# Key/value tiles inside the gated unit, query tiles in quarters inside attention, another load order, and the MLP's last up chunk moved off VectorE

## What is computed

```python
h = rms_norm(x, norm_mix_g)
z = h @ w_in                        # (B, S, 1024 q | 256 k | 256 v | 1024 value | 1024 gate)
q = rope(rms_norm(q, q_norm_g), pos);  k = rope(rms_norm(k, k_norm_g), pos)
a = attn(q, k, v, sinks)            # window of 128; the prompt in blocks of 128 queries
u = u_val * sigmoid(u_gate)         # gated unit
c = causal_dwconv(u, c_buf, conv_w, conv_b)          # 31 taps
c = silu(layer_norm(c, conv_ln_g, conv_ln_b))
x = x + concat(a, c) @ w_out
x = x + square(relu(rms_norm(x, norm_mlp_g) @ w_up)) @ w_down   # 2048 -> 8192 -> 2048
```

## Time and profile before

| | |
|---|---|
| median of 3 runs | 1556.63 us (1556.50 to 1557.89) |
| the profiled execution | 1554.67 us; span of its slowest core 1553.1 us |
| spans of the cores | 1545.5 to 1553.1 us, granted clock 0.963 to 0.967 |
| TensorE busy | 1409.0 us, 91% |
| VectorE, ScalarE, GpSimd busy | 688.5, 359.9, 267.0 us |
| last chain | TensorE 81%, VectorE 6%, ScalarE 3%, transfers 3% |

### The profile page before, as it was taken

The page is one execution under the profiler, slowest core; times in us unless marked ns, Lnnn a source line. Parts: engine busy times, 40 slices in busy tenths (PEclk is TensorE's granted clock), DMA queues, the critical chain, the costliest instruction groups (busy, mean ns, idle before and its releaser), DMA issues.

```text
span 1553.1 us, 22041 instructions; the slowest of 8 cores (1545.5 to 1553.1 us)
## 1 busy us (share of the span) xinstructions
PE 1409.0 (91%) x9006; PEld 868.7 (56%) x9006; DVE 688.5 (44%) x770; ACT 359.9 (23%) x516; POOL 267.0 (17%) x260
## 2 busy tenths in 40 slices
PE   4589978776989899999999999999999999999996
PEld 2356643332226555566666666666666666666664
DVE  2556634465331211253453453463463463463464
ACT  3356675344772222101001001001001001001000
POOL 0577712646000000101001001001001001001000
PEclk9899999889899999999999999999999999999998
DMA  9556420310453343745245255245245246246309
GB/s 247 127 82 109 82 41 5 50 12 28 110 122 55 55 71 52 122 82 90 47 82 92 46 82 95 42 82 96 40 82 97 40 82 97 40 82 101 60 17 217
DMA packets 52517, 122.75 MB, mean 79 GB/s; under 512 B 19215, under 2 KB 22543, under 8 KB 52395
## 3 DMA queue, kind: packets, MB, share of 16 engines
q0 software_dynamic: 43888, 91.07, 36.4%
q1 hardware_dynamic: 8531, 30.28, 6.9%
HBM read 203.42 MB, written 10.35 MB: 138 GB/s over the span
## 4 chain that ended last, share of the span: by engine, by line
PE 81%; DVE 6%; ACT 3%; issue 3%; DMA 3%; SPq 1%; POOL 1%; DVEq 0%; ACTq 0%; POOLq 0%
PE psum L529 81%; DVE arena L501 5%; ACT arena L497 2%; DMA arena<-xu 2%; ACT arena L691 1%; SPq L484 1%; DVE arena L673 1%; DMA arena<-wup 1%; POOL arena L501 1%; DVE arena L516 0%; PE psum L533 0%; ACT arena L515 0%; DVE arena L606 0%; DVEq L262 0%; DVE arena L522 0%
## 5 line engine op out<-in xcount | busy, mean ns | idle before, releaser
L529 PE MATMUL psum<-arena 128*128 128x343 bf16 (+7 forms) x8880 | 1398.4, 318 | 99.6 <-DVE arena L501 59.3
L529 PEld LDWEIGHTS psum<-arena 128*128 128x128 bf16 (+2 forms) x8880 | 859.4, 99 | 632.6 <-issue 183.7
L501 DVE TENSOR_TENSOR arena<-psum,arena 128x1029 f32<-128x1029 f32 (+9 forms) x396 | 397.4, 1019 | 302.8 <-PE psum L529 263.0
L501 DVE TENSOR_TENSOR arena<-arena 128x1029 bf16<-128x1029 bf16 (+5 forms) x160 | 175.3, 1095 | 371.5 <-ACT arena L497 363.6
L497 ACT ACTIVATE arena<-psum 128x1029 bf16<-128x1029 f32 (+8 forms) x157 | 121.1, 773 | 835.1 <-PE psum L529 832.4
L501 POOL TENSOR_TENSOR arena<-arena 128x256 f32<-128x256 f32 (+8 forms) x58 | 155.3, 2684 | 139.2 <-DVE arena L501 85.9
L484 POOL DMA_DIRECT2D arena<-wup x64 | 33.9, 530 | 817.1 <-PE psum L529 817.0
L497 ACT ACTIVATE arena<-arena 128x512 f32<-128x512 f32 (+13 forms) x181 | 121.2, 694 | 217.7 <-DVE arena L501 123.2
L673 DVE TENSOR_TENSOR arena<-psum,arena 32x264 bf16<-32x264 f32 x128 | 78.5, 613 | 58.6 <-PE psum L529 54.9
L691 ACT ACTIVATE arena<-psum,arena 32x256 f32<-32x256 f32 x128 | 91.1, 712 | 46.5 <-PE psum L529 43.4
L522 DVE TENSOR_REDUCE arena<-arena 128x4 f32<-128x256 bf16 (+4 forms) x20 | 16.3, 817 | 75.3 <-ACT arena L497 75.2
(11 more groups left out here) (13 smaller groups left out, 26.8 us busy)
## 6 DMA issues: line engine op xcount, KB each, us to landing
arena<-wup POOLq DMA_DIRECT2D x64, 512.0 KB, 6.7
arena<-wdn POOLq DMA_DIRECT2D x64, 512.0 KB, 13.8
arena<-xu SPq DMA_DIRECT2D x16, 530.0 KB, 23.3
arena<-xt SPq DMA_DIRECT2D x16, 514.0 KB, 5.7
yt<-arena SPq DMA_DIRECT2D x16, 514.0 KB, 9.2
arena<-wu POOLq DMA_DIRECT2D x16, 512.0 KB, 6.2
arena<-wo POOLq DMA_DIRECT2D x16, 512.0 KB, 6.2
arena<-wq POOLq DMA_DIRECT2D x16, 256.0 KB, 6.0
```

Of the source, the lines that this page charges most:

```text
L501: return P.add(eng, lambda e: e.tensor_tensor(out=out.ap, in0=in0.ap, in1=in1.ap, op=op), reads=[in0, in1], writes=[out])
L529: return P.add("pe", lambda e: e.matmul(out.ap, lhsT.ap, rhs.ap, start=start, stop=stop), reads=[lhsT, rhs], writes=[out])
```

## The change

- **Start.** The third and fourth weight blocks wait for x 10 and x 13. The first value block is copied to the f32 tile `V0` by ScalarE, and `glu_mul(0)` reads that. The four key/value weight loads move ahead of the loop.
- **Gated unit.** `glu_mul` comes in two halves with a K/V tile between them. In channel c, from 2 on: first half of `glu_mul(c-1)`, `kv_tile(c-2)`, second half, the gate's matmuls, the transposes `kv_tr(c-2)`, `glu_gate(c)`, `conv(c-1)`, the bands for c + 1, the value's matmuls. In channel 1, GpSimd's order is: SG product, K tables, bands 1, bands 2, Q tables. The chain is split into `chain1` (square, products, reduction, first sum) and `chain2` (root and the last products).
- **Between.** K/V tiles 6 to 9, `conv(7)` with its second half taken out by VectorE, query tile 9, cache loads, the `cvs` transfers on SP, `u_outputs` (its state transposes in two batches), query tiles 1 and 2 with the first layer norm statistic. `UTO`, `LB8`, `LSQ8`, `SGL`, `PT` and `REC` have new places.
- **Attention.** In block n: scores, a quarter of query tile n + 3, values and denominators, a quarter, the unit's end, one channel's layer norm, and the same for the second unit. Scores have three banks in a ring. The samples' attention goes in three pieces after blocks 2, 3 and 4, the sigmoids after blocks 5 and 6, `ln_mul` with the load of its `XT` tile after block 6 and at the end; then `XT` 8 to 15 are loaded, and the memset of `XT` follows.
- **Output projection.** All squares on ScalarE; the 16 contraction steps go in the order CT 0 to 3, AT 0 to 3, CT 4 to 7, AT 4 to 7.
- **MLP.** A group's last up chunk is squared on ScalarE and scaled on GpSimd; the down weights of a group are issued one by one with its up chunks.

The diff, cut:

```diff
-    SGL = [sb(O_XU + 14624 + 2080 * i, BF16, (NM,)) for i in range(8)]
+    SGL = [sb(O_XU + 12576 + 2080 * i, BF16, (NM,)) for i in range(4)]
+    PT = [sb(O_XU + 23584 + 1024 * i, BF16, (4, 128)) for i in range(8)]
+    REC = sb(O_XU + 31776, F32, (4, 128))
-    UTO = sb(O_XU + 8480, F32, (8, 128))
+    UTO = sb(O_XU + 18080, F32, (8, 128))
-    LB8 = sb(O_XU + 17696, BF16, (8, 343))
-    LSQ8 = sb(O_XU + 23200, BF16, (8, 343))
+    LB8 = sb(O_XU + 12576, BF16, (8, 343))
+    LSQ8 = sb(O_XU + 18080, BF16, (8, 343))
+    V0 = sb(O_TMP + 5952, F32, (NCOL,))
...
-    load_wu(after=[xl[8]])
-    load_wu(after=[xl[11]])
+    load_wu(after=[xl[10]])
+    load_wu(after=[xl[13]])
...
+    cp("act", lin352(V0), main3(av))
+    cp("act", V0((NU, NCOL)), av(2, (352, 356)))
...
+    for c in range(1, 8):
+        if c >= 2:
+            glu_mul(c - 1, acc3(1), 0)
+            kv_tile(c - 2, 6)
+            glu_mul(c - 1, acc3(1), 1)
+        u_block(pending.pop(0), acc3(0))
+        if c == 1:
+            halo_stats()
+            col_stats()
+        else:
+            kv_tr(c - 2, 7)
+        glu_gate(c, acc3(0))
+        load_wu()
+        if c == 1:
+            tt("pool", GCK(), TABIN(0), bc(GK, 1, (128, 10, 64)), ALU.mult)
+            tt("pool", GSK(), TABIN(1), bc(GKS, 1, (128, 10, 64)), ALU.mult)
+        conv(c - 1) if c >= 2 else None
+        if c == 1:
+            build_bands(1)
+        elif c + 1 < 8:
+            build_bands(c + 1) if c >= 2 else None
+        u_block(pending.pop(0), acc3(1))
+        if c == 1:
+            conv(0)
+            build_bands(2)
+            tt("pool", GCQ(), TABIN(0), bc(GQ, 1, (128, 10, 64)), ALU.mult)
+            tt("pool", GSQ(), TABIN(1), bc(GQS, 1, (128, 10, 64)), ALU.mult)
+        load_wu()
...
     def ln_mul(c):
-        tt("dve", CT(c), CC(c), SGL[c](), ALU.mult)
+        tt("dve", CT(c), CC(c), SGL[c % 4](), ALU.mult)
+        dma("sp", XT(c, (0, NX)), R(xt_d[c]), "xr%d" % c)
...
+    glu_mul(7, acc3(1), 0)
+    kv_tile(6, 0)
+    glu_mul(7, acc3(1), 1)
+    kv_tile(7, 1)
+    kv_tr(6, 2)
+    kv_tile(8, 0)
+    kv_tr(7, 2)
+    conv(7)
+    kv_tile(9, 1)
+    kv_tr(8, 2)
...
+    q_part(9, 3, 0, 16)
+    kv_tr(9, 2)
...
+    dma("pool", CKB(p=(0, 127)), R(ck[:, 1:128, :].rearrange("s k d -> k s d")), "cks", group=True)
+    dma("pool", CVB(p=(0, 127)), R(cv[:, 1:128, :].rearrange("s k d -> k s d")), "cks", group=True)
+    for s_ in range(SPC):
+        dma("sp", CVB(s_, p=(127, 128)), VB_S(p=(s_, s_ + 1)), "cvs", group=True)
+    q_chain1(9)
+    q_chain2(9)
+    u_outputs()
+    q_part(1, 0, 0, 16)
+    q_tr(9)
+    q_chain1(1)
+    ln_cast(0)
+    q_chain2(1)
+    q_part(2, 3, 0, 16)
+    ln_stats(0)
+    q_tr(1)
+    q_chain1(2)
+    ln_cast(1)
...
+    for n in range(8):
+        qn = n + 3 if n + 3 <= 8 else None
+        u0, u1 = 2 * n, 2 * n + 1
+        sc(u0)
+        if qn:
+            q_part(qn, 0, 0, 4)
+        if n == 0:
+            ln_stats(1)
+        if n + 2 <= 8:
+            q_chain2(n + 2)
+        pv(u0)
+        if qn:
+            q_part(qn, 0, 4, 8)
+        unit_b(u0)
+        if n == 0:
+            ln_cast(2)
+        elif n >= 2:
+            ln_step(2)
+        sc(u1)
+        if qn:
+            q_part(qn, 0, 8, 12)
+        if n + 2 <= 8:
+            q_tr(n + 2)
+        if n == 0:
+            ln_stats(2)
+        pv(u1)
+        if qn:
+            q_part(qn, 0, 12, 16)
+        unit_b(u1)
+        if n >= 1:
+            ln_step(2 if n < 6 else 2)
+        if qn:
+            q_chain1(qn)
...
+    for c in range(4, 8):
+        ln_mul(c)
+    for k in range(8, 16):
+        dma("sp", XT(k, (0, NX)), R(xt_d[k]), "xr%d" % k)
     memset("pool", XT((0, 16), (NM - 1, NM)), 0.0)
...
-        if dc % 4 != 3:
-            act(sq((0, 1024)), XT(dc, (0, 1024)), AF.Square)
-        else:
-            tt("dve", sq((0, 1024)), XT(dc, (0, 1024)), XT(dc, (0, 1024)), ALU.mult)
+        act(sq((0, 1024)), XT(dc, (0, 1024)), AF.Square)
...
+    korder = [8, 9, 10, 11, 0, 1, 2, 3, 12, 13, 14, 15, 4, 5, 6, 7]
...
+            wdq[g].append(wdn_load(g * GFF + fi))
...
-            tt("dve", hid(fi), hid(fi), hid(fi), ALU.mult)
-            tt("dve", hid(fi), hid(fi), RS2f(), ALU.mult)
+            if fi == GFF - 1:
+                act(hid(fi), hid(fi), AF.Square)
+                tt("pool", hid(fi), hid(fi), RS2f(), ALU.mult)
+            else:
+                tt("dve", hid(fi), hid(fi), hid(fi), ALU.mult)
+                tt("dve", hid(fi), hid(fi), RS2f(), ALU.mult)
```

More of the change, by code:

```diff
@@ L662, in glu_gate, with glu_mul @@
         tt("pool", SG(), SG(), RS(), ALU.mult)
-    def glu_mul(c, accv):
+    def glu_mul(c, accv, half):
         u = UP[c % 2]
-        for j in range(4):
+        for j in (2 * half, 2 * half + 1):
             pj = (32 * j, 32 * j + 32)
@@ new lines, in kv_tr, with u_block @@
+    def kv_tr(ti, bank):
+        tn, c0, nt = TT[ti]
+        fin_qk(K2[ti % 3], 2, KT, bank, c0, nt)
+    def u_block(w, acc):
+        for kc in range(16):
+            for pi, (a, b) in enumerate(PU):
+                mm(acc(pi, (0, b - a)), w(kc), HT(kc, (a, b)), kc == 0, kc == 15)
+    for k4 in range(2):
+        load_wkv(k4)
+    load_wu()
+    load_wkv(2)
+    load_wu()
+    load_wkv(3)
+    glu_gate(0, ag)
+    build_bands(0)
+    glu_mul(0, av, 0)
+    glu_mul(0, av, 1)
+    halo_norm()
@@ L899, in build_program, with q_part @@
-    while pend:
-        fin_qk(*pend.pop(0))
+        tt("dve", CT(c), CC(c), SGL[c % 4](), ALU.mult)
+        dma("sp", XT(c, (0, NX)), R(xt_d[c]), "xr%d" % c)
+    qstate = {}
+    def q_part(ti, bank, a, b):
+        tn, c0, nt = TT[ti]
+        pp = (0, nt)
+        accq = ps_f32(bank, 2, (16, 64))
+        for kc in range(a, b):
+            for hf in range(2):
+                mm(accq((8 * hf, 8 * hf + 8), p=pp), tile_l(kc, ti), WQ(kc, (512 * hf, 512 * hf + 512)),
+                   kc == 0, kc == 15)
+        if b == 16:
+            qbt = QKBufs()
+            qbt.SQ, qbt.B = qb.SQ, qb.B
+            qbt.A = qb.A if ti % 2 == 0 else qb.A2
+            qstate[ti] = (accq, 16, nt, GCQ, GSQ, ti, qbt)
@@ new lines, in unit_b, with samp_k @@
+    def unit_b(ui):
+        n, gp = units[ui]
+        own_c0 = 128 * n
+        cs = (gp * 4, gp * 4 + 4)
+        pso = ps_f32(6, 1, (4, 128))
+        psd = ps_f32(7, 1, (4, 128))
+        rec = REC
+        tt("dve", rec(), psd(), bc(ESK(cs), 2, (128, 4, 128)), ALU.add)
+        act(rec(), rec(), AF.Ln)
+        act(rec(), rec(), AF.Exp, scale=-1.0)
+        tt("dve", AT(cs, (own_c0, own_c0 + 128)), pso(), rec(), ALU.mult)
+    ptk3 = None
+    def samp_k():
+        ptk = ps_bf16(2, (8, 128))
+        for s_ in range(SPC):
+            for c in range(2):
+                tr(ptk(2 * s_ + c, (0, 127)), CKB(s_, (128 * c, 128 * c + 128), p=(0, 127)),
+                   IDB((0, 127), p=(0, 127)))
+        ptk3 = Buf("ps", ptk.ap.rearrange("p (s c) k -> p s c k", c=2), ptk.off, (SPC, 2, 128), 2)
+        cp("act", KTS((0, SPC), (0, 2), (0, 127)), ptk3((0, SPC), (0, 2), (0, 127)))
+        ktn = KT((0, 2), (SC0, SC0 + SPC))
+        cp("dve", Ref(KTS.ap[:, :, :, 127], KTS().rngs), Ref(ktn.ap.rearrange("p c s -> p s c"), ktn.rngs))
@@ new lines, in samp_pv @@
+    def samp_pv():
+        psos = ps_f32(6, 1, (8, SPC))
+        psds = ps_f32(7, 1, (8, SPC))
+        for s_ in range(SPC):
+            for g in range(4):
+                pr = (64 * (g % 2), 64 * (g % 2) + 64)
+                cs = ((g // 2) * 4, (g // 2) * 4 + 4)
+                rhs = PTS((16 * s_ + 4 * g, 16 * s_ + 4 * g + 4))
+                mm(psos(cs, (s_, s_ + 1), p=pr), CVB(s_, (64 * g, 64 * g + 64)), rhs, True, True)
+                mm(psds(cs, (s_, s_ + 1), p=pr), ONB((0, 64)), rhs, True, True)
+        tt("dve", RECS(), psds(), bc(ESK(), 2, (128, 8, SPC)), ALU.add)
+        act(RECS(), RECS(), AF.Ln)
+        act(RECS(), RECS(), AF.Exp, scale=-1.0)
+        tt("dve", AT((0, 8), (1024, 1024 + SPC)), psos(), RECS(), ALU.mult)
@@ L1035, in build_program, with ln_step @@
-    act(RECS(), RECS(), AF.Ln)
-    act(RECS(), RECS(), AF.Exp, scale=-1.0)
-    tt("dve", AT((0, 8), (1024, 1024 + SPC)), psos(), RECS(), ALU.mult)
-    memset("pool", AT((0, 8), (NM - 1, NM)), 0.0)
+    lnq = []
+    for c in range(8):
+        lnq += [(ln_norm1, c), (ln_norm2, c)]
+    def ln_step(k=1):
+        for _ in range(k):
+            if lnq:
+                f, c = lnq.pop(0)
+                f(c)
+    for n in range(8):
[31 more added lines that the diff above has]
+            q_chain1(qn)
+        if n == 2:
+            samp_k()
+        if n == 3:
+            samp_s()
+        if n == 4:
+            samp_pv()
+        if n == 5:
+            while lnq:
+                ln_step()
+            for c in range(4):
+                ln_sig(c)
+        if n == 6:
+            for c in range(4):
+                ln_mul(c)
+            for c in range(4, 8):
+                ln_sig(c)
@@ L1039, in build_program @@
+    for c in range(4, 8):
```

(7 more changed lines are left out.)

354 lines of the change are left out of this document (137 added, 217 removed).

## The result

| | before | forecast | after |
|---|---|---|---|
| median | 1556.57 us | 1593.6 (1562 to 1620) | 1601.95 us |
| profiled execution, span | 1554.67, 1553.1 | 1591.7 | 1603.6, 1602.0 |
| end of the last value block, M | 203.6 | 235.5 | 240.1 |
| M to the first scores, L | | 84 | 87.2 |
| L to the last quarter's end, E | | 154 | 157.9 |

The changed kernel is slower: 1.0283 of the kernel before, with an interval of 1.0258 to 1.0308. The forecast was slower by 2.4%; the 11.9 us that the profiled execution took beyond the sum are made of +4.6 up to M, +3.2, +3.9, +2.9 and -2.8.

The account below looks back on a forecast made before the run. It took in-order queues in front of small chains, from the key/value stage through attention, as the bound. +61 up to the first output matmul and -24 behind it gave +37: 1591.7, or 1593.6 us on the median's scale, range 1562 to 1620.

Parts of the forecast that it names:

- A. Start: Kernel start: third and fourth unit weights issued two arrivals of x later; 3 us off, bounds 0 and 5.
- B. First two channels: Ahead of kv_tr(0): TensorE stands some 18 us for GpSimd's cast; +8 with the start's gain, bounds 0 and +13.
- C. Gated unit: Five steady channels at 23.2 instead of 18.43 us, VectorE's chain showing 0.9 us each time; +24.
- D. From M to L: Last value block to first scores: SP waits for the CVB load, ScalarE behind it; 84 us, bounds 61 and 87.
- rival 1: Between M and L: CVB lands before UTO is copied, so scores at M + 61 and time 1571; chance 0.14.
- E. The loop: Attention blocks: ScalarE's in-order chain gives 24.2 us a block; sum 145 plus 9 for the clock, 154 us.
- Rival 2: Attention loop: all bursts run at half speed, 36 instead of 9 us; time 1621; chance 0.13.
- Rival 3: Attention loop runs at TensorE's pace, blocks 2 to 5 at 15.5 instead of 24.2 us; time 1539; chance 0.08.
- F. Tail: Last quarter to first output matmul: the first output weight is queued behind the XT memset; 54 us (50 to 60).
- O: Mark for the first output matmul, forecast at 527.5 against 466.4 before, +61.
- G. Behind O: Output projection -8, MLP -15, spreading of down weights' loads counted as 1; -24, bounds -20 and -27.
- Rival 4: Parts cancel: half of SP's wait (-12), blocks at 20 us (-17), no slow clock (-9); time 1556; chance 0.05.

Follow-up runs that it names:

- e1_cvs: Changed kernel with the four cvs transfers on SP moved behind u_outputs and its transfers out of UTO; 1581.43 us, 1.0185 of the kernel before.
- e3_ln: Changed kernel with each channel's layer norm pieces placed behind the next unit's scores and exponentials; 1564.79 us, 1.0076 of the kernel before.
- e6_back: Kernel before with only the squares moved to ScalarE and the last up chunk's square and scaling off VectorE; 1532.64 us, 0.9871.

## Why the forecast held, step by step

**A. Start: too hopeful.** The sum had -3; the last row of x's loop comes only 0.55 us earlier than before (51.92). That is 2.5 of the 7.5 us missed up to the end of channel 2's value block (119.5 forecast, 127.0 by the 99 matmuls from 113.04, of which 84 belong to it).

**B. First two channels: right wait, wrong start.** GpSimd's list took 85.29 to 112.65, 27.4 us, where the sum had 30.3 with its three handovers. But it began at 85.3, not at 75.6. The 7.2 us beyond A are V0: the sum took off the wait of the earlier trace rows and did not put on that `glu_mul(0)` now has both inputs in SBUF, with GpSimd's bands beside it. The Trainium skill's page "SBUF — State Buffer", section "Who interferes with whom", says that such a VectorE instruction and a GpSimd instruction that reads SBUF exclude each other for a whole instruction, by order of issue; the 8.25 us piece, which ends when the bands do, agrees, and so does the same work from PSUM in 10.16 us. The forecast quoted that rule for the layer norm pair and missed it where the change moves an operand. This is the one step whose mechanism was left out. The wait for the cast was there, but it was 9.0 us and not 18: TensorE came to it later, held up by the two waits in front of it.

**C. Gated unit: right.** From 127.0 to 240.1 are five channels, 22.6 us each against 23.2. TensorE waits 0.2 to 0.5 us for the K chain where the sum had 0.9.

**D. From M to L: right, by two misses that cancel.** The CVB load began at M + 39.9, 6.3 us later than in the sum, and landed in 30.2 us, not in the 38.9 of the earlier trace rows: faster, but not by half. In the kernel before, the cache copies are issued beside it, here behind it; that this is the reason is not shown. ScalarE's square came at M + 75.5, forecast M + 75; rival 1 (M + 61) is out. Its price was wrong too: without SP's wait, in e1_cvs, the scores came 71 us after the last value block, so the other work was put 10 us too low (its terms as written add up to 60).

**E. The loop: right in sum, the clock's share too small.** Blocks 2 to 5 with the sample's pieces took 110.9 us (374.3 to 485.2) against 97 + 3 and 9 for the clock; blocks 0 and 1 took 47.0 against 45. Inside the sum two misses cancel, and that part is luck. The eleven matmuls behind the two gaps of a block took 4.96 and 4.17 us, where they take 2.64 at full clock, so half clock costs 3.8 us of the 27.55; over the eight gaps of the four blocks it is 16 us, where I took 9 for the whole loop. The chain without it is 94.8 us for the four blocks instead of 97 + 3, and 23.7 in the block shown instead of 24.2 (the terms as written add up to 23.8). Rival 2 named a real effect at too high a price. Rival 3's condition, scaling not ahead of the exponentials, is e3_ln: its blocks took 18.2 to 22.6 us, not 15.5. The Trainium skill's page "TensorE: Matmul & The Clock Gate", section "HAM oscillation — how this bites in real kernels", has bursts restart at half clock after idle gaps; the gaps of 4.06 us here agree, and behind the gap of 0.30 us in e3_ln the same matmuls ran at the speed of full clock. That the forecast read a gap of 2.81 us as free does not carry over: behind 2.95 and 2.60 us in e3_ln they ran slowly.

**F. Tail: right.** 56.9 against 54. The memset came at E + 43.8, where the sum had the last product's end at E + 43. The first weight was to land 10 us after its issue with twelve loads beside it; from its issue at 529.7 to O it took 12.4.

**G. Behind O: right in sum, one step wrong.** -26.8 against -24; the waits for VectorE went, as forecast. Wrong was that GpSimd's product delays only a load that is wanted late: at the first crossing of e6_back the load behind it is the one that TensorE waits for, 10.2 us; at the others the step was right. Where the down weights are spread, a guess of 1 us, neither that wait nor the 2.9 us of the kernel before is left; that the spreading does it is not shown by itself.

Rival 4, that the parts cancel, needed half of SP's wait and blocks of 20 us; neither came.
